# Fused attention and state-space network on one core: projection blocks of the attention in order of use, ropes, norms and splits done among them, output norms inside the head loop

## The reference, cut to what matters

```python
h = rms_norm(x, pre_norm[l])
proj = h @ w_in[l]                      # 24 tiles of 128 columns
(dq, dk, dv, dgate, gq, gk, gv, ggate, mq, mgate) = split(proj)
dq, dk = rope(dq), rope(dk)             # 6 heads, two halves of 32 each
oa = softmax(q1 k1) v - lam * softmax(q2 k2) v        # differential heads
oa = rms_norm(oa, diff_subln[l]) * (1 - lambda_init) * silu(dgate)
gq, gk = axial_rope(rms_norm(gq)), axial_rope(rms_norm(gk))
ob = softmax(gq gk * 0.125) gv * silu(ggate)          # 6 grouped heads
mk, mv = split(rms_norm(mem) @ w_mem_kv[l])           # 256 memory rows
om = softmax(mq mk * 0.125) mv * silu(mgate)          # 4 memory heads
y = concatenate([oa, ob, om]) @ w_out[l]
x = x + rms_norm(y, post_norm[l])
```

## Time and profile before

| | |
|---|---|
| three runs | 3060.99, 3062.64 (median), 3070.03 us |
| profiled execution, its own time | 3068.31 us |
| its span in the profile | 3066.5 us |
| PE busy | 2799.9 us (91%) |
| DVE busy | 1653.3 us (54%) |
| ACT busy | 1156.3 us (38%) |
| POOL busy | 449.2 us (15%) |
| chain that ended last | PE 76%, DVE 10%, issue 4%, ACT 3%, DVEq 3%, POOLq 2% |

### The profile page before, as it was taken

How to read it: one execution, slowest core, us unless ns; L and a number is a source line. 1 busy time by engine, 2 the same in 40 slices (tenths; PEclk the granted TensorE clock), 3 DMA queues, 4 the chain that set the end, 5 groups by cost and what they waited for, 6 DMA issues and landing times.

```text
span 3066.5 us, 37070 instructions
## 1 busy us (share of the span) xinstructions
PE 2799.9 (91%) x13972; PEld 2299.9 (75%) x13972; DVE 1653.3 (54%) x2427; ACT 1156.3 (38%) x1943; POOL 449.2 (15%) x383
## 2 busy tenths in 40 slices
PE   6987978978979999989699999999999997899998
PEld 5855767845768888888578888888888885788887
DVE  4469755379756543375536443264432697554423
ACT  3237843237834432222324222242222565432222
POOL 1011001020017830024302000010000212200000
PEclk9987989987999999987699999999999998899999
DMA  3320002220014332342222222332223210123222
GB/s 129 96 82 1 1 28 85 97 68 1 1 34 119 132 117 82 99 133 70 64 81 81 85 95 84 95 97 84 94 84 94 83 56 28 56 83 96 87 87 74
DMA packets 292400, 234.80 MB, mean 77 GB/s; under 512 B 43683, under 2 KB 286060, under 8 KB 291756
## 3 DMA queue, kind: packets, MB, share of 16 engines
q1 hardware_dynamic: 289180, 219.49, 23.5%
q10 hardware_dynamic: 2016, 7.46, 0.8%
q0 software_dynamic: 1072, 6.10, 0.6%
HBM read 220.83 MB, written 12.19 MB: 76 GB/s over the span
## 4 chain that ended last, share of the span: by engine, by line
PE 76%; DVE 10%; issue 4%; ACT 3%; DVEq 3%; POOLq 2%; POOL 1%; SPq 0%; DMA 0%; ACTq 0%
PE bank L376 23%; PE bank L378 22%; PE bank L377 22%; DVE WL L362 2%; PE bank L1566 1%; ACT WH L357 1%; DVE stats L1870 1%; PE bank L1553 1%; PE bank L1578 1%; DVE XL L434 1%; DVE CV L1126 1%; POOLq L2318 1%; DVEq L1871 1%; POOLq L2316 1%; DVE E L1897 1%
## 5 line engine op out<-in xcount | busy, mean ns | idle before, releaser
L376 PE MATMUL bank<-XH,WH 128*128 128x512 f32 (+1 forms) x2688 | 996.8, 371 | 79.2 <-DVE WL L362 25.4
L378 PE MATMUL bank<-XH,WL 128*128 128x512 f32 (+1 forms) x2688 | 988.4, 368 | 0.0
L377 PE MATMUL bank<-XL,WH 128*128 128x512 f32 (+1 forms) x2688 | 986.7, 367 | 0.0
L362 DVE TENSOR_TENSOR WL<-raw,WH 128x2048 fp32r<-128x2048 f32 (+1 forms) x212 | 447.8, 2112 | 558.1 <-ACT WH L357 557.7
L376 PEld LDWEIGHTS bank<-XH,WH 128*128 128x128 f32 x2688 | 516.6, 192 | 176.6 <-issue 37.5
L357 ACT ACTIVATE WH<-raw 128x2048 fp32r<-128x2048 f32 (+1 forms) x212 | 370.0, 1746 | 581.6 <-PE bank L378 581.6
L377 PEld LDWEIGHTS bank<-XL,WH 128*128 128x128 f32 x2688 | 517.3, 192 | 90.0 <-issue 1.0
L378 PEld LDWEIGHTS bank<-XH,WL 128*128 128x128 f32 x2688 | 516.1, 192 | 87.8
L378 PE MATMUL bank<-HH,WL 128*128 128x512 f32 (+1 forms) x792 | 293.4, 371 | 0.0
L376 PE MATMUL bank<-HH,WH 128*128 128x512 f32 (+1 forms) x792 | 293.3, 370 | 0.0
L377 PE MATMUL bank<-HL,WH 128*128 128x512 f32 (+1 forms) x792 | 292.7, 370 | 0.0
(11 more groups left out here) (379 smaller groups left out, 3599.8 us busy)
## 6 DMA issues: line engine op xcount, KB each, us to landing
raw<-in_ffn_w_dram SPq DMA_DIRECT2D x88, 1024.0 KB, 5.3
raw<-in_ffn_w_dram SPq DMA_DIRECT2D x64, 704.0 KB, 4.6
raw<-in_w_in_dram SPq DMA_DIRECT2D x24, 1024.0 KB, 5.2
raw<-in_w_out_dram SPq DMA_DIRECT2D x8, 1024.0 KB, 5.1
raw<-in_cv_w_in_dram SPq DMA_DIRECT2D x8, 1024.0 KB, 5.4
cs_scr<-CSA ACTq DMA_DIRECT2D x8, 520.0 KB, 3.0
raw<-in_w_mem_kv_dram SPq DMA_DIRECT2D x4, 1024.0 KB, 5.4
raw<-in_s_w_in_dram SPq DMA_DIRECT2D x4, 1024.0 KB, 7.7
```

What stands on the lines that cost most here:

```text
L362: dve.tensor_tensor(WL[:, slot, 0:n * P], raw[:, slot, 0:n * P], WH[:, slot, 0:n * P].bitcast(F32), ALU.subtract).then_inc(l_done, 1)
L376: pe.matmul(out, WH[:, slot, c:c + P], h, start=start, stop=False)
L377: pe.matmul(out, WH[:, slot, c:c + P], l, start=False, stop=False)
L378: return pe.matmul(out, WL[:, slot, c:c + P], h, start=False, stop=stop)
```

## The change

1. `BLOCKS` sets another order of the twelve projection blocks: differential queries and keys first, then grouped queries and keys, then values and the rest. `SP`, `split_h` and `split_l` follow it.
2. The `swap` matmuls, the transposes of values and the head squares stand between or in the middle of blocks (`middle`), and the DVE's `turn` (rope), `value_low`, `head_norm` and ACT's `value_high`, `lead_qk`, `silu` stand between the splits of weights. The rope table is loaded earlier, and some buffers have other places.
3. The norm of heads takes the logarithm and an exponential on ACT in place of root and DVE reciprocal. The scale of the scores is multiplied into the queries beforehand (`QSCALE`, `headg`), so that `maxima` writes the negated maximum itself (`negate=True`) and line 1872 falls away.
4. `E` has 8 slots. The scaling of units 24 to 63 is done by POOL in place of ACT.
5. The output norms of the differential heads lie at unit 48 of the head loop, the splits of the output tiles at units 53 to 58 and 66, and weight block 15 is split at unit 50.
6. In `turn_act` two squares come after `yrms_act`. In `in_pair` the two small matmuls of the last stage stand before steps 3 and 6 in place of 2 and 5.

```diff
+        BLOCKS = [(0, 1), (2, 3), (4, 5), (6, 7), (12, 13), (14, 15), (8, 9), (16, 17), (20, 21), (10, 11),
+                  (18, 19), (22, 23)]
+        SLOTS = 8
+        MIX_AT = {53: 0, 54: 1, 55: 2, 56: 3, 57: 4, 58: 5, 66: 6}
+        SQUARE_AT = {33: 0, 35: 1, 37: 2}
...
         def attn_pool(pool, s):
...
+            for u in range(DIFF_UNITS, len(UNITS)):
+                m, nk = SCORE0[u], HEADS[UNITS[u][0]][2]
+                pool.wait_ge(ss(s, "rsum"), at(s, "rsum", u + 1))
+                e = E[:, m % SLOTS, 0:nk * P]
+                pool.tensor_tensor(e, e, stats[:, 3, m % 8:m % 8 + 1].to_broadcast([P, nk * P]), ALU.mult)\
+                    .then_inc(ss(s, "pn"), 1)
             out_pool(pool, s)
...
         def attn_pe(pe, s):
...
+            block(5)
+            swap(2)
+            swap(3)
+            pe.wait_ge(ss(s, "vml"), at(s, "vml", 1))
+            value_turn(0)
             head_squares(0)
+            block(6, lambda: head_squares(1))
+            swap(4)
+            swap(5)
+            value_turn(1)
             head_squares(2)
+            block(7, lambda: head_squares(3))
+            value_turn(2)
+            block(8, lambda: (swap(6), swap(7)))
+            value_turn(3)
+            block(9, lambda: (swap(8), swap(9)))
+            block(10)
+            block(11)
...
+            def output_norms():
+
+                for n in range(3):
+                    m = NORM_M + n
+                    pe.wait_ge(ss(s, "osq"), at(s, "osq", n + 1))
+                    pe.wait_ge(ss(s, "e"), at(s, "e", m - 3))
+                    pe.matmul(bank[m % 4][:, :], perm[:, 1, :], norm_buf(n), start=True, stop=True)\
+                      .then_inc(ss(s, "s"), 1)
...
         def attn_dve(dve, s):
...
+            turn(2)
+            turn(3)
+            evict(6)
+            low_w(10)
+            value_low(1)
+            turn(4)
+            turn(5)
+            evict(7)
+            low_w(11)
+            value_low(2)
+            for n in range(4):
+                head_norm(n)
...
             for u in range(len(UNITS) + LAG_V + 1):
                 if u < len(UNITS):
                     maxima(u)
+                if u == 51:
+                    low_w(15)
                 if 2 <= u < DIFF_UNITS + 2:
                     combine(u - 2)
...
+                if NORM_U + 2 <= u < NORM_U + 5:
+                    output_norm(u - NORM_U - 2)
+                if u - 1 in MIX_AT:
+                    mix_low(MIX_AT[u - 1])
+            mix_low(KD - 1)
...
         def turn_act(act, s, sqr, evict, b, step, n1, middle=None):
...
-            square(act, nxt_s, 0, n1 - 2)
+            square(act, nxt_s, 0, 2)
             yrms_act(act, s, 1)
+            for k in range(4, n1):
+                square(act, nxt_s, 0, k - 1)
             split_h(act, b + 1, 1, 16, step)
```

529 lines of the change are left out of this document (285 added, 244 removed).

## The result

The changed kernel takes 2989.61 us (median of four runs, 2988.40 to 2992.76); the kernel before, on the same chip, 3064.56 us (3060.99 to 3070.03). The ratio is 0.9755, with a 95% interval of 0.9738 to 0.9773. The forecast was 2985 us, with a range of 2950 to 3020. The same kernel measured again on another chip gave 0.9743 [0.973, 0.9756].

What follows compares the result with a forecast made beforehand. PE, busy for 91% of the span, bounds the kernel. Per attention 40.3 - 13.4 + 5.3 + 4.6 = 36.8 us, two 73.6, seams 3.9: 77.5 off 3068.3 gives 2990.8, as a median 2985 us; range 2950 to 3020.

Steps and rivals of the forecast that it cites:

- Start of the heads: Last projection block to first exponential: of 42.9 us only 2.6 (read-out, silu, table load) stay, gain 40.3 us per attention.
- rival (e): Gap before the heads only changes place, first scores waiting for something late; 35 of each 40.3 us kept, 3055 us; chance 0.03.
- Blocks: Projection blocks: swaps 8.6, transposes 2.4, head square 0.9 and waits 1.5 move in; cost 13.4 us per attention.
- rival (c): PE waits among the blocks, each of five swap groups 3 us late; 33 us more in all, 3018 us; chance 0.20.
- Differential units: 24 units of the head loop: 0.22 us less each from line 1872 and more slots, 5.3 us per attention (3 to 9).
- the two more slots: Differential units: two more slots of `E` spare exponentials the wait for transposes, for which ACT waited 5.6 us over 20 units.
- rival of a larger gain (b): Heads' loop gains more, differential units at 2.95 us, memory units lose 7, seams give 8 more: 2950 us; chance 0.20.
- Grouped and memory units: Head loop: grouped units unchanged as PE paces; memory units 35.5 to 36 us for 22.3, loss 13.5 (7 to 18) per attention.
- The holding by POOL: Memory units: POOL's operations hit VectorE's 14 added operations about every third time; with waits in the chain, 6.5 us.
- Rival (d): POOL's scaling paces grouped and memory units; at 4.5 us per 128x512 tile the kernel gets slower, 3104 us; chance 0.04.
- Gap and low clock: Ahead of the output projection: the 17.1 us wait goes; of 2.7 us for the low clock behind it, 1 comes back.
- Seams: Between stages: four seams gain 6.3 us, feed-forward seams lose 2.4; net gain 3.9 us, bounds a loss of 2.4 and 16.

Runs made afterwards that it cites:

- e1: Changed kernel with the first attention's tiny state-space parameter chains moved early and ScalarE's wait for their end removed: 2982.03 us, ratio 0.971.
- e8: Changed kernel with output norms at unit 36 for 48, five output splits at units 41 to 47, last weight split at 38 and 39: 2986.4 us, ratio 0.9738.
- e6: Changed kernel with six buffers for the exponentials instead of eight: 2987.69 us, ratio 0.9743.
- e3: Changed kernel with the three output norms and all eight splits of the output projection's input moved behind the unit loop: 3016.61 us, ratio 0.9827.
- e5: Changed kernel with both seam edits taken back (order of leads and squares, places of the small norm matmuls): 2995.43 us, ratio 0.9769.
- e2: Changed kernel with one more, overwritten matmul ahead of each score accumulation of the 24 differential units: 2996.83 us, ratio 0.9752.
- e10: Changed kernel with a tiny multiply by one and its drain put back behind each unit's reductions on VectorE: 3007.42 us, ratio 0.9792.
- e13: Changed kernel with the output norms' logarithm and exponential replaced by plain copies, so without two function table loads: 2993.34 us, ratio 0.9771.
- e9: Changed kernel with both the early parameter chains of e1 and the norms at unit 36 of e8: 2980.56 us, ratio 0.9716.
- e11: Changed kernel with the early parameter chains of e1 and only the last weight split at units 38 and 39 for 50 and 51: 2994.05 us, ratio 0.9759.

## Why the prediction was right, point by point

**Start of the heads (-40.3).** Right in the second attention to 0.2 us, and the three operations behind the last block are those named. In the first it was 6.2 us short, for the cause that rival (e) names, the tiny chains of the state-space parameters. The step that failed is that I gave this rival the whole gap or nothing, and took -40.3 for both attentions. e1 shows the place of the chains, with ScalarE's wait for their end, to be the cause.

**Blocks (+13.4).** +11.5 and +12.8. PE was busy for 112.19 of 112.80 us, so the waits for ropes and norms, put at 1.5 us, were 0.6, and rival (c) didn't occur.

**Differential units (-5.3).** This is the mis-sized term: +0.3 and -2.6. The operation that fell away is worth about what I said while the clock is as it was: at 0.79 and 0.80 (e8) 20 units took 63.4 and 62.3 us, 3.4 to 4.5 less than the 66.8 at 0.81 of before. But the clock wasn't as it was: at 0.76 they took 65.8, at 0.70 68.6. "The low clock in this part I leave as it is" was the wrong step, and the prediction's own sign of being wrong, a clock other than 0.81 there, came. Over the runs with this code the time goes with the low time: 24.9 us of it with 62.3, 26.6 with 63.4, 31.6 with 65.8 and 41.2 with 68.6, from one end to the other 0.39 us more for each us of it, and more at the lower end. (The low time is worked out from the length, and no run sets the clock by itself, so this is a relation and no proof.) DVE's busy time is 57.5 to 57.9 us in all of them, so that its idle time grows from 4.8 to 10.9 us; TensorE's idle time stays at 7.5 to 8.9. So DVE doesn't pace these units alone, as the prediction said; TensorE's speed does beside it. And the second reason given, the two more slots, is refuted by e6. The rival of a larger gain (b) counted on 2.95 us for a unit; at the measured clocks it is 3.1 to 3.4.

**Grouped and memory units (0 and +13.5).** +8.6 and +8.8 together. The boundary was misread by four units, as said above. With the true one the prediction's working gives even more: VectorE's 21.2 us less 2.7, its added work of 10.9, 5 dry and 6.5 of waits are 40.9 us in place of 29.6. Measured, TensorE's idle time from unit 44 on grew by 4.2 us (2.9 to 7.1), near the 5, though behind the 48th exponential; the six matmuls of the norms are 2.6 us, and the rest, some 1.8 us, goes mostly by the lower clock. VectorE's work was sized right, 7.7 us more (21.19 to 28.91) for 8.2. What was too dear is that it was taken to add in full: VectorE had 8.4 us of idle time in these units before and has 4.0 after. The holding by POOL, a part of the 6.5 us, was small: the products took 0.95 us for 0.69 and the seven low parts of the outputs 0.74 for 0.62, 1.6 us in sum. Maxima and low parts of the transposed tiles took 0.41 and 0.42 us beside POOL as without it, so that not everything on VectorE is held. Rival (d), POOL as pacer, had its price at 1.04 us, not 4.5, and TensorE waited for it for 0.2 us.

**Gap and low clock (-17.1, -1).** The gap went whole. Of the low clock 2.5 us came back, not 1: PE had 7.5 us of work in the last 8.8 us of the loop. e3 gives the size of the output norms' place as a whole: some 13 us in the second attention, of which 2.5 us are idle time of TensorE and the rest goes by its clock.

**Seams (-3.9).** 5.4 us by the difference of the two traces, 7 to 9 by e5. The four waits for the sum of squares fell by 12.0 us in sum (24.9 to 12.9), of which not all is gain, as other waits grew. That the small matmul stands a step later at the feed-forward seams costs what was said: TensorE's wait there went from 3.8 to 4.5 us at each of the three, 0.7 us for the 0.8 of the sum. (The upper bound of 16 us was added up wrongly: two thirds of 25.4 us are 17.)

**What stays open.** No run puts swaps, transposes and ropes back behind the last block, so the largest term rests on the two traces. Why the clock fell more often in the differential units than before: before, it was 0.81 in both attentions, after, 0.70 and 0.76 (0.70 to 0.80 over all traces with this code), though TensorE had the same matmuls in about the same time. What decides between 0.90 and 0.54 in the memory units (e2, e10) wasn't found; these two kernels have no edit of TensorE's or ScalarE's work there. The same program gives different clocks in its two attentions, in one run (e13); whether the time at which a stage starts takes part is a guess that no run tests. The versions with the norms at 36 or 48 can't be told apart under this.

The fastest versions are those with the parameters' chains early, e1 (0.971 [0.9692, 0.9728]) and e9 (0.9716 [0.97, 0.9732]), which can't be told apart.

## What to carry to other kernels

Look at what stands in a queue that belongs to another stage: tiny operations of 0.2 us made the start of the heads 6.3 us late, because some took 1.2 us beside GpSimd, and the read-out and ScalarE's last silus stood behind the rest. Moved to an earlier place they cost nothing that can be seen (the blocks end at 213.4 to 214.5 us in the runs with that edit, at 212.3 to 214.9 in those without). Idle time of an engine in a stage isn't room for work as long as the stage's chain goes through that engine's queue: a weight split of 2.3 us on VectorE made eight units 3.0 us longer, although VectorE was busy for only two thirds of them (e11). A stretch between two exponentials that gets longer isn't yet a loss either: look whether TensorE was idle in it. And where TensorE runs at a mixed clock, read the clock's row with each time and forecast a range: its two levels went with 6 us in 65 for one unchanged piece of code, more than most edits in it.

## What was not expected of the hardware

The granted clock of unchanged code differs from run to run and between the two attentions of one run: 20 differential units at 0.70 to 0.80 took 68.6 to 62.3 us, and 16 memory units at 0.90 or 0.54 took 32.9 and 40.7 us. A tiny VectorE operation on 128x64 elements took 1.14 to 1.21 us beside GpSimd's 128x512 operations, and 0.20 to 0.23 alone.

A change of ScalarE's function table cost 1.28 us, and the activation behind it started at once (352.90 and 354.19). The Trainium skill, ScalarE: Activation LUTs (section What ACT_TABLE_LOAD costs), puts a switch at 1.28 us and 1.38 for a drain; the load agrees, a drain doesn't show in this trace, and taking two loads away (e13) brought the next exponential 2.0 us sooner and the kernel nothing.
